# Projecting the first two weight tiles per token group while the input is still being transposed, with more input buffers and a later, two-pass gate product

## The reference: what is computed

```python
hn = rmsnorm(x, norm1[l])
proj = hn @ w_in[l]                     # 3080 columns
xr, yr, qkv_raw, z, rest = jnp.split(proj, SPLITS[:4], axis=-1)
b_raw, a_raw = rest[..., :GDN_HEADS], rest[..., GDN_HEADS:]     # 4 + 4 gate columns
xc, rc_new = causal_conv(xr, ...)       # RG-LRU branch, 512 channels
gate_r = sigmoid(xc @ w_a + b_a); gate_i = sigmoid(xc @ w_i + b_i)   # blocks of 64
log_a = -RG_C * gate_r * softplus(-lam)
h = scan(exp(log_a), sqrt(-expm1(2 log_a)) * gate_i * xc);  out_rg = gelu(yr) * h
beta = sigmoid(b_raw)
g = -exp(gdn_A_log) * softplus(a_raw + gdn_dt_bias)
# then conv and silu of q|k|v, the gated delta rule, w_out, and a SwiGLU FFN
```

## Time and profile before

| what | us |
|---|---|
| median of three runs | 1606.57 |
| the profiled execution | 1607.14 |
| its span | 1605.4 |
| PE busy over the span | 1525.1 (95%) |
| DVE, ACT, POOL busy | 720.5, 351.1, 131.8 |
| mean granted TensorE clock | 0.984 |
| PE busy from 0 to 100 us | 78.06 |
| PE busy from 100 to 200 us | 93.50 |

### The profile page before, as it was taken

How to read it: one execution, slowest core, us unless ns; L and a number is a source line. 1 busy time by engine, 2 the same in 40 slices (tenths; PEclk the granted TensorE clock), 3 DMA queues, 4 the chain that set the end, 5 groups by cost and what they waited for, 6 DMA issues and landing times.

```text
span 1605.4 us, 22937 instructions
## 1 busy us (share of the span) xinstructions
PE 1525.1 (95%) x8959; PEld 1395.4 (87%) x8959; DVE 720.5 (45%) x1157; ACT 351.1 (22%) x569; POOL 131.8 (8%) x200
## 2 busy tenths in 40 slices
PE   5999999998999999998899999999999999999996
PEld 3798899997888888886698989989898989989895
DVE  5345554534566665664434243342424243342416
ACT  5353523331111111111030201111020201111012
POOL 1000000001222222112000000000000000000001
PEclk9999999998999999999899999999999999999999
DMA  5011222263122112212270102011010102010002
GB/s 195 14 43 56 81 92 80 90 187 101 41 66 65 58 40 65 65 57 68 79 282 27 53 27 78 26 52 52 26 52 26 52 26 78 26 52 26 0 0 111
DMA packets 52561, 105.12 MB, mean 65 GB/s; under 512 B 4784, under 2 KB 30320, under 8 KB 52528
## 3 DMA queue, kind: packets, MB, share of 16 engines
q1 hardware_dynamic: 52528, 104.67, 18.9%
HBM read 82.66 MB, written 22.00 MB: 65 GB/s over the span
## 4 chain that ended last, share of the span: by engine, by line
PE 44%; issue 2%; DVE 2%; ACT 1%; DMA 1%; POOL 0%; DVEq 0%; ACTq 0%; POOLq 0%
PE bank L86 14%; PE bank L87 14%; PE bank L88 14%; ACT gu_hi L1605 1%; DVE acc L1697 1%; PE bank L1593 1%; DMA out_y<-y_out 1%; DVE y_out L1657 0%; DVE hf L1669 0%; PE bank L1594 0%; PE bank L1591 0%; ACT y_out L1643 0%; DVE acc L1703 0%; POOL fstat L1718 0%; DVEq L1696 0%
## 5 line engine op out<-in xcount | busy, mean ns | idle before, releaser
L86 PE MATMUL bank<-ht_hi,w_hi 128*128 128x364 f32 (+1 forms) x576 | 190.1, 330 | 1.0 <-DVE w_lo L543 1.0
L1669 DVE TENSOR_TENSOR hf<-sg,bank 128x364 f32<-128x364 f32 (+1 forms) x66 | 35.1, 531 | 343.5 <-PE bank L88 342.8
L88 PE MATMUL bank<-ht_hi,w_lo 128*128 128x364 f32 (+1 forms) x576 | 189.1, 328 | 0.0
L87 PE MATMUL bank<-ht_lo,w_hi 128*128 128x364 f32 (+1 forms) x576 | 188.9, 328 | 0.0
L86 PE MATMUL bank<-ht_hi,gu_first_hi 128*128 128x364 f32 (+1 forms) x528 | 174.1, 330 | 1.4 <-PEq L842 1.4
L87 PE MATMUL bank<-ht_lo,gu_first_hi 128*128 128x364 f32 (+1 forms) x528 | 174.3, 330 | 0.0
L88 PE MATMUL bank<-ht_hi,gu_first_lo 128*128 128x364 f32 (+1 forms) x528 | 174.0, 329 | 0.0
L88 PE MATMUL bank<-ht_hi,gu_lo 128*128 128x364 f32 (+1 forms) x528 | 173.5, 329 | 0.0
L86 PE MATMUL bank<-ht_hi,gu_hi 128*128 128x364 f32 (+1 forms) x528 | 173.3, 328 | 0.0
L87 PE MATMUL bank<-ht_lo,gu_hi 128*128 128x364 f32 (+1 forms) x528 | 173.3, 328 | 0.0
L1697 DVE TENSOR_TENSOR acc<-acc,bank 128x512 f32<-128x512 f32 x198 | 132.7, 686 | 81.0 <-PE bank L88 76.4
(11 more groups left out here) (277 smaller groups left out, 2493.6 us busy)
## 6 DMA issues: line engine op xcount, KB each, us to landing
w_raw<-in_w_in SPq DMA_DIRECT2D x24, 512.0 KB, 4.2
dn_raw<-in_w_down SPq DMA_DIRECT2D x22, 512.0 KB, 4.2
scratch_qkv<-cb_y SPq DMA_DIRECT2D x12, 512.0 KB, 2.7
qkv_in<-scratch_qkv SPq DMA_DIRECT2D x8, 768.0 KB, 6.3
gu_first_raw<-in_w_gate SPq DMA_DIRECT2D x11, 512.0 KB, 3.5
gu_first_raw<-in_w_up SPq DMA_DIRECT2D x11, 512.0 KB, 4.4
gu_raw<-in_w_gate SPq DMA_DIRECT2D x11, 512.0 KB, 3.6
gu_raw<-in_w_up SPq DMA_DIRECT2D x11, 512.0 KB, 4.3
```

Of the source, the lines that this page charges most:

```text
L86: pe.matmul(out, w_hi, x_hi, start=start, stop=False)
L87: pe.matmul(out, w_hi, x_lo, start=False, stop=False)
L88: return pe.matmul(out, w_lo, x_hi, start=False, stop=stop)
L1669: eng.tensor_tensor(hf[b][:, 0:m], sg[b][:, 0:m], psum[2 * b + 1][:, 0:m], ALU.mult).then_inc(hf_done, 1)
```

## The change

- `xin` gets four buffers and `xn` three, the squares go to a scratch tile of their own, and `in_stat` has a column pair per tile. SP's first loads are x0, the constants, x1, weight tile 0, x2, x3, weight tile 1, then the rest of x, all other constants, and last the gate weights (`gate_w_in`).
- The transposes go to banks 6 and 7 for even tiles, 2 and 5 for odd ones. PE's order becomes: transposes of x0 to x3; group 0 of weight tile 0; x4, x5; group 0 of tile 1; x6, x7; group 1 of tile 0; x8; group 1 of tile 1; group 2 of tile 0; gate products 0 and 1; group 2 of tile 1.
- `w_lo` of the first two weight tiles is made on POOL (`low_first`), after its root of x3 and of x6; `w_hi` on ACT after `high(1)` and `high(4)`.
- A gate product is 16 matmuls a group: high and low gate weights lie side by side (16 columns) against `ht_hi`, the high ones alone against `ht_lo`. `turn_gates` adds the two halves by a product with a 16 x 8 pattern (`sum8`, new columns of `expo`). The third gate product stands behind project(2), `turn_gates` behind the first group of project(3).
- The pair's gate matmuls of pairs 1 to 3 are spread: the two of group 0 ahead of the last token group of project(2j+1), the rest behind it. Those of pair 0 come before project(2).
- Softplus of `lambda` stays on DVE; that of `g` moves to POOL (`gate_decays`, 24 dependent steps) and ACT (`gate_values`), within pair 1.

The core of the diff:

```diff
+            load_x(1)
+            eng.dma_start(w_raw[0][:, :, :], i["w_in"][0]).then_inc(w_in[0], 16)
+            load_x(2)
+            load_x(3)
+            eng.dma_start(w_raw[1][:, :, :], i["w_in"][1]).then_inc(w_in[1], 16)
+            for m in range(NX, MT):
+                load_x(m)
...
             def gates(n):
                 a, m = GROUPS[n]
+                out = psum[6 + n % 2]
                 for f in range(KT):
-                    mm = mm3(eng, psum[5 + n][0:2 * H, 0:m], gw_hi[:, f, :], gw_lo[:, f, :],
+                    eng.matmul(out[0:4 * H, 0:m], gw[:, f, :], ht_hi[:, f, a:a + m], start=f == 0, stop=False)
+                    if f == KT - 1:
+                        break
+                    eng.matmul(out[0:2 * H, 0:m], gw[:, f, 0:2 * H], ht_lo[:, f, a:a + m], start=False, stop=False)
...
+            def turn_gates():
+                eng.wait_ge(gt_done, 3)
...
+            def early(t, n):
+                eng.wait_ge(w_hi_done, t + 1)
+                eng.wait_ge(w_lo_done, t + 1)
+                eng.wait_ge(xt_free, -(-sum(GROUPS[n]) // P))
+                group(t, t, n)
...
             def rg_tile(j):
                 project(2 * j, 0)
-                project(2 * j + 1, 1)
+                project(2 * j + 1, 1, lambda n: rg_gates(j, n - 1) if n >= 1 else None)
+                rg_gates(j, 2)
...
+            project(2, 0)
+            eng.wait_ge(rg_tanh, 6)
+            gates(2)
...
+            project(3, 1, after)
...
+            for m in range(MT):
+                if m + 2 < MT:
+                    square(m + 2)
+                high(m)
+                if m in (1, 4):
+                    split_first(m // 4)
...
                 split_next(2 * j, 0, j + 2)
+                if isinstance(j, int) and j == 0:
+                    evac_gates(0)
+                    evac_gates(1)
+                if isinstance(j, int) and j == 1:
+                    gate_values()
...
+            def low_first(t):
+                eng.wait_ge(w_hi_done, t + 1)
+                eng.tensor_tensor(w_lo[t][:, :, :], w_raw[t][:, :, :], f32(w_hi[t][:, :, :]),
+                                  ALU.subtract).then_inc(w_lo_done, 1)
+            for m in range(MT):
+                norm_tile(m)
+                if m in (3, 6):
+                    low_first(m // 6)
```

More of the change, by code:

```diff
@@ L198, in input_block @@
     VEC = 11
+    RG_ARG, G_ARG, G_DONE = 3, 2, 26
     PAIRS = QKV // 2
@@ L332, in project @@
-            def project(t, s):
+                out = psum[6 + n % 2]
+                for f in range(KT):
+                    eng.matmul(out[0:4 * H, 0:m], gw[:, f, :], ht_hi[:, f, a:a + m], start=f == 0, stop=False)
+                    if f == KT - 1:
+                        break
+                    eng.matmul(out[0:2 * H, 0:m], gw[:, f, 0:2 * H], ht_lo[:, f, a:a + m], start=False, stop=False)
+                eng.matmul(out[0:2 * H, 0:m], gw[:, KT - 1, 0:2 * H], ht_lo[:, KT - 1, a:a + m],
+                           start=False, stop=True).then_inc(gate_proj, 1)
@@ new lines, in turn_gates, with group @@
+            def turn_gates():
+                eng.wait_ge(gt_done, 3)
+                for m in range(MT):
+                    n = rows_of(m)
+                    mm = eng.matmul(psum[7][0:n, m * 2 * H:(m + 1) * 2 * H], gt[:, m * P:m * P + n],
+                                    sum8[0:4 * H, :], start=True, stop=True)
+                mm.then_inc(gate_proj, 1)
+            def group(t, s, n):
+                a, m = GROUPS[n]
+                for f in range(KT):
+                    mm = mm3(eng, bank(s, n)[:, 0:m], w_hi[s][:, f, :], w_lo[s][:, f, :],
+                             ht_hi[:, f, a:a + m], ht_lo[:, f, a:a + m], f == 0, f == KT - 1)
+                mm.then_inc(proj, 1)
@@ new lines, in project, with rg_gates @@
+            def project(t, s, between=None):
+                eng.wait_ge(w_hi_done, t + 1)
+                eng.wait_ge(w_lo_done, t + 1)
+                eng.wait_ge(evac_done, t - 1)
+                for n in range(len(GROUPS)):
+                    group(t, s, n)
+                    if between:
+                        between(n)
+            def rg_gates(j, n):
+                a, m = GATE_GROUPS[n]
+                if n == 0:
+                    eng.wait_ge(rg_conv, 4 * (j + 1))
+                    eng.wait_ge(gate_w_in, 16 * (j + 2))
+                for q in range(2):
+                    if not (isinstance(j, int) and j == n == q == 0):
+                        eng.wait_ge(rg_tanh, 6 * j + max(0, 2 * n + q - 1))
+                    eng.matmul(psum[6 + q][:, 0:m], rg_w[:, q, :], rb_xc[:, a:a + m],
+                               start=True, stop=True).then_inc(gate_mm, 1)
@@ L359, in _ @@
-            loop(eng, R, rg_tile)
-            eng.wait_ge(g_done, 2)
+                project(2 * j + 1, 1, lambda n: rg_gates(j, n - 1) if n >= 1 else None)
+                rg_gates(j, 2)
+            for m in range(4):
+                transposes(m)
+            early(0, 0)
+            transposes(4)
+            transposes(5)
+            early(1, 0)
+            transposes(6)
+            transposes(7)
+            early(0, 1)
+            transposes(8)
+            early(1, 1)
+            early(0, 2)
@@ L362, in _ @@
+            project(3, 1, after)
+            rg_gates(1, 2)
+            with eng.Fori(2, R) as j:
+                rg_tile(j)
+            eng.wait_ge(g_step, G_DONE)
             eng.wait_ge(more_in, NMORE)
```

343 lines of the change are left out of this document (180 added, 163 removed).

## The result

The changed kernel takes 1616.22 us (median of 4 runs, 1615.13 to 1616.91), beside 1605.02 for the kernel before in the same session (4 runs, 1603.33 to 1607.94). The ratio is 1.0067, 95% interval 1.0049 to 1.0086: slower by 0.7%. The forecast was about 1606 us, which can't be told from no change, with a range of 1599 to 1613. The time lies above the range, and the interval lies above 1, so the slowdown is real. The profiled execution took 1616.91 us with a span of 1615.1, 9.7 longer than before. Two later runs at a far lower mean clock (one of e2, 2161.17 us at 0.652, and one of the kernel before, 1907.09 us at 0.746) are left out of all comparisons.

A forecast was written before the change was run, and what follows sets the result against it. PE was taken as the bound, busy 95% of the span, with the loss at the start. The terms -15.0 + 10.6 + 0.8 + 2.9 = -0.7 us on 1607.14 gave 1606.4, as median about 1606, range 1599 to 1613.

The forecast's parts named there:

- First milestone: End of pair 0's last gate matmul: forecast at 65.9 us instead of 80.88, 15.0 us won.
- Rival 3: At the start, POOL's subtraction runs at its slow bound, 4.2 us later at tile 1: 1610.2 us, chance 0.10.
- Wait before `turn_gates`: In pair 1, PE idles 4.4 us for ACT's copy, behind a rounding whose load stands behind SP's store.
- It turns (0.7): In pair 1, PE's turning of the gate products was to take 0.7 us.
- Pair 1's clock charge: Low clock after the 4.4 us of idle in pair 1, charged at 2.0 us.
- Pairs 2 and 3: Each to take 32.4 us, against 31.58 and 29.55 before: +0.8 and +2.85 us.
- From the last on, the program is the same.: Behind the fourth pair's last gate matmul (171.37 us before) nothing changes, so the end moves as that milestone does.
- the term for the clock: Charges for low clock after new idle stretches: 2.0 at the start, 2.0, 0.6 and 0.6 in the pairs, together 5.2 us.
- Rival 2: The clock falls in all seven new idle stretches, costing 12.6 us instead of 5.2: 1613.4 us, chance 0.20.
- Rival 4: The start isn't filled, groups wait for tiles anyway; 5 us won there, 14 lost in the pairs: 1616 us, chance 0.04.
- A's 12: Low end of the 12 to 17.5 us that the part up to project(2) was to win.
- B: The part on the lengths of pairs 1 to 3, where the change loses 10.6, 0.8 and 2.9 us.

The follow-up runs named there:

- e2: The changed kernel with ACT's rounding of weight tile 1 behind the copies of x3 instead of x4: 1607.67 us, ratio 1.0022 to before.
- e1: The changed kernel with ACT's copy of the third gate product ahead of its rounding of weight tile 4: 1606.55 us, ratio 1.0020 to before.
- e10: The changed kernel with SP's weight loads for the next pair ahead of the store of rb_gy: 1606.95 us, ratio 1.0020 to before.
- e3: The changed kernel with all gate matmuls of pairs 1 to 3 behind the second weight tile again: 1604.28 us, ratio 0.9996 to before.
- e12: The kernel before with only SP's weight loads for the next pair ahead of the store: 1599.74 us, ratio 0.9971 to before.
- e5: e4 with ACT's rounding of weight tile 2j+3 behind the six tanh in each pair: 1590.25 us, ratio 0.9903 to before.
- e7: e4 with two buffers each for xin and xn, as before the change: 1594.78 us, ratio 0.9933 to before.
- e8: The kernel before with only the gate products in two passes, 16 instead of 24 matmuls a group: 1601.57 us, ratio 0.9983 to before.
- e11: e6 with SP's weight loads for the next pair ahead of the store, as in e10: 1589.67 us, ratio 0.9910 to before.
- e4: The changed kernel with the edits of e1, e2 and e3 together: 1590.76 us, ratio 0.9914 to before.
- e6: e4 with the low parts of the first two weight tiles made on DVE instead of POOL: 1589.56 us, ratio 0.9902 to before.
- e9: The changed kernel with the edits of e4, e6, e5 and e10 together: 1584.43 us, ratio 0.9883 to before.

## Why the prediction was wrong

The forecast for the profiled execution was 1606.4, and 1616.9 came: 10.5 us. Step by step:

- **First milestone, 65.9 forecast, 68.89 measured (+3.0).** The mechanism was right: PE idled before tile 1's first group, 4.15 us for 3.7, up to the end of POOL's late subtraction (29.77 + 3.22; the wait is listed as "issue"). The sizes failed. The first weight group began at 20.97 for 19.6, since DVE's scaling of x3 stood behind POOL's first subtraction; the second one began 1.3 us later than forecast and took 3.22 us for 2.6. That makes 2.0 us at 33.10. The other 1.0 is the clock: from 33.10 the low level cost PE 3.0 us instead of 2.0. The prediction also had a case in which contention with DVE makes each subtraction 1.3 us later: the first lost nothing, the second 0.85, and DVE lost 2.0, which no case had. Rival 3 had the right place and, for POOL, too high a price.
- **Wait before `turn_gates`, 4.4 us forecast, 3.86 measured.** Right, by its chain too; e1 and e10 each removed it.
- **"It turns (0.7)".** Wrong by 3.2 us. The price was that of nine transposes; the new form is 18 instructions, 2.15 us at full clock and 3.88 at the low one.
- **Pair 1's clock charge, 2.0.** Wrong: the fall from 90 cost PE 1.7 in the turning and 2.6 in the group behind, and a second fall, not charged at all in this pair, made its last matmuls 4.28 us instead of 3.06. With the turning's own 1.5 and 0.5 less of waiting this makes pair 1 44.40 us instead of 39.95: 1.7 + 2.6 - 2.0 + 1.2 + 1.5 - 0.5 = 4.5.
- **Pairs 2 and 3, 32.4 each, measured 32.20 and 33.61 (-0.2, +1.2).** The waits were 1.33 and 1.71 us for the convolution (forecast 1.65) and 2.02 behind the last group (forecast 2.15). Charged was 0.6 for the clock in each; it fell in pair 3, for 1.4 us, and not in pair 2. So the average was off in each pair and right in their sum, which with two cases is luck.
- **"From the last on, the program is the same."** It was, but its time was not: 1436.0 us instead of 1434.0 (+2.0). A fall from 182, just behind the small decay matmuls, cost about 1.5. What remains can't be put down to the change. Counted from the last milestone, the mixer's first transposes began 1.3 us later than before:

```profile
369.74 1.94 PE L964 MATMUL bank<-cst,qkv_in 128*128 128x128 f32 x8 [3.90 <-PEq L212]
378.74 1.94 PE L1079 MATMUL bank<-cst,qkv_in 128*128 128x128 f32 x8 [3.90 <-PEq L226]
```

(The first row is before's, the second after's.) The FFN began 3.2 later; in the mixer between them the clock loss was 10.2 us (from 376) where before it was 6.8 (from 369). The FFN took 1.2 less. All this is within what the traces differ by in this part.

The sum is 3.0 + 4.5 - 0.2 + 1.2 + 2.0 = 10.5. Every stall of the argument was there at about its length. The step that failed is the term for the clock. 5.2 us were charged, and PE lost 11.4: 3.0 before the first milestone, 4.3 and 1.2 in pair 1, 1.4 in pair 3 and 1.5 behind the decay matmuls. That is 6.2 of the 10.5; next come the start with 2.0 (POOL and DVE in each other's way) and the turning with 1.5. The long stop before `turn_gates` was charged at 2.0 and cost 4.3, the stop behind the last group of pair 1 at nothing, and the fall behind the decay matmuls stood in no rival.

Rival 2, the clock falling in the new stretches, comes nearest: it said 1613.4. Of its seven stops four had a fall, at 3.0, 4.3, 1.2 and 1.4 us for its 2.8, 2.8, 1.4 and 1.4. The fifth fall was at a place that it didn't name. Rival 4's 1616 is the number that came, but not its way: it had the start unfilled, and the first milestone came 12.0 us earlier. The range was also cut short: its own terms, A's 12 with rival 2's falls in B (-12 + 8.6 + 0.2 + 2.25 + 9.8 on 1606.57), give 1615.4 and not 1613. The Trainium skill (TensorE: Matmul & The Clock Gate, section "Why this matters for your kernels") spoke for rival 2. The trace agrees at the stops of 4.15 and 3.86 us, which both had a fall; of the three of 2.02 us two had one.

e3's surplus belongs to the same term. Of the clock loss it took away (6.9 us, 13.7 less 6.8), the falls at 110 and 175 are 3.4; the one at 182 and half of that at 32 are the other 3.4, and the edit doesn't touch these places. Part of what e3 won is thus not shown to be the spreading's own. In pairs 1 to 3, where it acts, it took off 9.4 us.

## What to carry to other kernels

When work is pulled forward to fill a start, follow every queue that the moved step now stands in: here a copy of 0.44 us stood behind a rounding that stood behind a load that stood behind a store, and moving either the copy or the load took 6.4 us off that pair. Price each new idle stretch of PE as idle time plus a fall of the clock, as a case of its own and not as an average, at the price of a row behind a stop of the same length. Spread matmuls into a dense row only where their inputs are ready by then. Price a new form of an instruction by its own count, and a new neighbour of DVE on POOL by what the one that starts second loses.

## What was not expected of the hardware

- Low clock came in equal portions. The clock loss of every fall from 28 to 200 us, over all fourteen traces, was 1.7, 3.4 or 5.1 us, and of that at the start of the mixer 6.8, 8.5 or 10.2. Behind idle times of 2.02 to 2.04 us it fell at nine stops (after at 110 and 175, two each in e1, e2 and e10, before at 137) and not at six (after at 142.43, before at 76.29, one each in e1, e2, e10 and e12). Behind waits of 0.8 to 1.8 us for tanh it never did. It also fell with PE fully busy: behind `turn_gates` in its new form without a wait in front of it (from 88 in e1, 81 in e5, 85 in e7, 58 in e8, 87 in e10, 80 in e11). And it fell behind the decay matmuls, in front of which PE had waited 0.75 us (from 182 in after, 173 in e1 and e10, 172 in e2, 156 in e5, 155 in e11). In e4, e6 and e9 it fell at neither place. What decides is open: each is a single trace, and no run was made for it.
- A turning matmul of fp32 by 8 columns shows as two instructions, 2.15 us for 18 (0.12 each) at full clock, where a transpose of the same block before took 0.08.
- DVE's scaling and POOL's subtraction of 128x1024 elements hold each other up, and the one that begins second pays. In the seven traces in which the scaling began 0.10 to 0.12 us behind POOL it took 3.32 or 3.33 us; in the five in which POOL began 0.27 or 0.28 us behind the scaling, POOL took 3.21 or 3.22. Without the other the scaling takes 1.27 and POOL 2.37 or 2.38, and DVE alone does both in 1.27 + 1.22 (e6).
